# GpSimd takes the residual add of the combine stage, VectorE keeps the weighted sum and the gate

## The reference, cut to what matters

```python
out = jnp.zeros((T + 1, D), h.dtype).at[row_tok].add((yb * row_w[:, None]).astype(h.dtype))
...
x = x + gt2[:, None, :] * hier_moe(h2, router_grp_w[l], ...)
```

## Time and profile before

| what | value |
|---|---|
| median of three runs | 2645.95 us (2642.81 to 2648.5) |
| profiled execution | 2643.21 us |
| its span, first to last instruction | 2641.4 us |
| `combine`: first issue to the end of the span | 2564.4 to 2641.4 us |
| busy over the whole span | PE 90%, DVE 41%, ACT 29%, POOL 15% |

### The profile page before, as it was taken

The page is one execution under the profiler, slowest core; times in us unless marked ns, Lnnn a source line. Parts: engine busy times, 40 slices in busy tenths (PEclk is TensorE's granted clock), DMA queues, the critical chain, the costliest instruction groups (busy, mean ns, idle before and its releaser), DMA issues. The chain is left out here.

```text
span 2641.4 us, 67871 instructions
## 1 busy us (share of the span) xinstructions
PE 2384.7 (90%) x27948; PEld 1456.3 (55%) x27949; DVE 1095.7 (41%) x2600; ACT 761.1 (29%) x1879; POOL 389.9 (15%) x481
## 2 busy tenths in 40 slices
PE   6999999999996899999999997899999999999960
PEld 4787787877875667777776764332333323332220
DVE  1456565565654355555656556011111111111118
ACT  1444535445352123232232321121122212221212
POOL 1111211212111122121212210010110101100000
PEclk8999999999997899999999998799999999999985
DMA  9021211212118422222222222934545596999958
GB/s 342 19 87 49 97 49 69 77 49 97 49 71 330 167 94 90 106 90 106 74 97 91 91 74 89 419 148 192 209 142 231 200 363 247 387 387 388 391 217 365
DMA packets 54246, 451.84 MB, mean 171 GB/s; under 512 B 7884, under 2 KB 8944, under 8 KB 32528
## 3 DMA queue, kind: packets, MB, share of 16 engines
q1 hardware_dynamic: 37656, 391.25, 37.9%
q0 software_dynamic: 10656, 38.80, 3.8%
q10 hardware_dynamic: 5720, 18.66, 1.8%
HBM read 367.43 MB, written 87.56 MB: 172 GB/s over the span
## 5 line engine op out<-in xcount | busy, mean ns | idle before, releaser
L1833 PE MATMUL ps<-arena 128*32 128x512 f32 x4608 | 510.4, 600 | 26.4 <-DMA arena<-wex 26.4
L453 PE MATMUL ps<-arena 128*128 128x128 f32 x3072 | 354.8, 276 | 14.7 <-ACT arena L599 14.7
L453 PEld LDWEIGHTS ps<-arena 128*128 128x128 f32 x3072 | 349.3, 193 | 27.3 <-ACT arena L599 24.5
L1833 PEld LDWEIGHTS ps<-arena 128*32 128x32 f32 x4608 | 149.9, 111 | 379.9 <-issue 364.7
L1127 PE MATMUL ps<-arena 64*64 64x64 f32 x8704 | 298.0, 221 | 30.0 <-ACT arena L1362 9.5
L1127 PEld LDWEIGHTS ps<-arena 64*64 64x64 f32 x8704 | 276.9, 136 | 61.0 <-issue 60.3
L1847 PE MATMUL ps<-arena 128*32 128x512 f32 x2304 | 265.3, 601 | 8.9 <-DMA arena<-wex 7.9
L1272 PE MATMUL ps<-arena 128*128 128x512 f32 x480 | 222.0, 605 | 0.0
L2060 DVE TENSOR_TENSOR arena<-arena,ps 128x256 f32<-128x256 f32 x72 | 29.9, 415 | 462.3 <-ACT arena L1891 462.3
L468 PE MATMUL ps<-arena 128*128 128x512 f32 (+1 forms) x512 | 213.9, 555 | 0.0
L1891 ACT ACT_TABLE_LOAD x36 | 46.2, 1283 | 581.6 <-PE ps L1833 581.6
(11 more groups left out here) (350 smaller groups left out, 2871.9 us busy)
## 6 DMA issues: line engine op xcount, KB each, us to landing
arena<-wex SPq DMA_DIRECT2D x105, 2048.0 KB
mid<-arena SPq DMA_DIRECT2D x16, 2568.0 KB, 8.5
arena<-mid SPq DMA_DIRECT2D x16, 2568.0 KB, 9.8
arena<-ada SPq DMA_DIRECT2D x12, 2048.0 KB, 9.4
arena<-y SPq DMA_DIRECT2D x16, 1024.0 KB, 7.5
arena<-x SPq DMA_DIRECT2D x31, 512.0 KB, 5.8
arena<-x ACTq DMA_DIRECT2D x17, 512.0 KB, 10.3
arena<-w_in SPq DMA_DIRECT2D x4, 2048.0 KB, 39.5
```

The costliest lines, as they stand in the source:

```text
L453: mm = pe.matmul(bank[name][:, at:at + P], V["w_in"][g][:, kk, at:at + P], V["hT"][:, kk, :], start=(kk == 0), stop=(kk == KD - 1))
L1833: mm = pe.matmul(bank[("HA", "HB")[g]][rows[j], :], xT[:, kk, rows[j]], slot[j][:, at:at + 2 * FH], start=(kk == 0), stop=(kk == KD - 1))
```

## The change

The third operation of a tile moves from VectorE to GpSimd. VectorE's gated product goes to a new buffer of its own, `gated`, one for each of the four tiles in flight; these buffers lie in a part of SBUF that holds expert weights before and nothing in this stage.

The semaphore `gated` now tells that VectorE is done with `y0`, `y1` and `sum` of a tile. SyncE's loads and ScalarE's scaling wait for it where they waited for `summed`. GpSimd takes over the waits for x1 and for the store of tile t-4, and signals `summed`. VectorE waits for `summed` of tile t-4 before it writes `gated` again. The drain behind the gate goes.

```diff
+    W["gated"] = [W["slot"][FLIGHT // 2][:, PIECE + D * i:PIECE + D * i + D] for i in (1, 2, 3)] + [W["slot"][FLIGHT // 2][:, 2 * PIECE:2 * PIECE + D]]
...
                 if u:
-                    sp.wait_ge(S["summed"], t - FLIGHT + 1)
+                    sp.wait_ge(S["gated"], t - FLIGHT + 1)
...
                 dve.scalar_tensor_tensor(m["sum"], m["y1"], V["top_w"][:, 2 * t + 1:2 * t + 2], m["sum"], ALU.mult, ALU.add)
                 dve.drain()
-                dve.tensor_tensor(m["sum"], m["sum"], W["gt2"], ALU.mult)
-                dve.drain()
-                dve.wait_ge(S[f"x1_in{u}"], 16 * FLIGHT)
                 if u:
-                    dve.wait_ge(S[f"stored_out{b}"], 16 * u)
-                dve.tensor_tensor(m["res"], m["sum"], W["x1"][t], ALU.add).then_inc(S["summed"], 1)
+                    dve.wait_ge(S["summed"], t - FLIGHT + 1)
+                dve.tensor_tensor(m["gated"], m["sum"], W["gt2"], ALU.mult).then_inc(S["gated"], 1)
+
+        @block.gpsimd
+        def _(pool):
+            for t, b, u in tiles:
+                m = buf[b]
+                pool.wait_ge(S["gated"], t + 1)
+                pool.sem_inc(S["passed"], 1)
+                pool.wait_ge(S[f"x1_in{u}"], 16 * FLIGHT)
+                if u:
+                    pool.sem_inc(S["passed"], 1)
+                    pool.wait_ge(S[f"stored_out{b}"], 16 * u)
+                pool.tensor_tensor(m["res"], m["gated"], W["x1"][t], ALU.add).then_inc(S["summed"], 1)
...
             def scale(t, b, u):
                 act.wait_ge(S[f"y_in{b}"], 16 * u + 16)
                 if u:
-                    act.wait_ge(S["summed"], t - FLIGHT + 1)
+                    act.wait_ge(S["gated"], t - FLIGHT + 1)
```

More of the change, by code:

```diff
@@ L2075, in combine @@
     buf = [{n: w[:, D * i:D * i + D] for i, n in enumerate(("y0", "y1", "sum", "res"))} for w in W["flight"]]
+    for m, gated in zip(buf, W["gated"]):
+        m["gated"] = gated
     tiles = [(t, t % FLIGHT, t // FLIGHT) for t in range(NT)]
```

## The result

The changed kernel takes 2659.83 us (median of five runs, 2657.55 to 2662.81), the kernel before 2646.12 us in five runs beside it. The ratio is 1.0053, with a 95% interval of 1.0038 to 1.0068: about 14 us slower. Of the profiled executions, the span went from 2641.4 to 2655.7 us.

A forecast was written before the change was run, and what follows sets the result against it. VectorE was taken to bound combine at 3.86 us a tile. With exclusion, fifteen tiles at 4.56 us move the last add from 2638.25 to 2649.5, 11.2 us slower: median 2657 us, range 2648 to 2665.

The forecast's parts named there:

- The bound of before: Combine stage, first scaled tile on: VectorE's gate, add and weighted sum with drain set 3.86 us a tile.
- The exclusion: Combine: VectorE operations with two SBUF inputs and GpSimd's add block each other, the second waiting; forecast built on it 0.80.
- the second rival: Combine: only the plain product excludes GpSimd, the weighted sum doesn't; 2644 to 2649 us, centre 2646; chance 0.08.
- GpSimd's hold: Time GpSimd's 1024-column add blocks VectorE: 2.05 us, plus 0.14 until its end is seen; ends 1.91 and 2.38.
- The turns: Combine: VectorE and GpSimd alternate in an order differing within each pair of tiles; 9.11 us a pair, 4.56 a tile.
- The sum: Combine's end: fifteen tiles at 4.56 us put the last add's end at 2649.5, store 3.15 us; change costs 11.2 us.
- the first rival: Combine: no exclusion, GpSimd runs beside VectorE, DMA engines bound at 3.74 us a tile; 2644 us; chance 0.09.
- until 2630 the DMA engines are full: Combine before 2630 us: DMA engines at 413 to 426 GB/s, so a tile costs at least 3.74 us.

## Why the prediction was right

**The bound of before** (VectorE at 3.86 us a tile) was right: the run with the early release alone leaves VectorE's list and keeps the time.

**The exclusion** was the step that decided, and it was read from three rows of another stage and their sixteen repeats. Shown: the long sorts appear in the changed kernel on all three lines; they go when the second input of VectorE's operations leaves SBUF, and the time goes with them. The rule of the Trainium skill (SBUF — State Buffer, Who interferes with whom) holds, for the weighted sum too, which the rows of before couldn't show: it lasted up to 3.12 us. The block ends some 0.2 us ahead of the profiled end of GpSimd's add (2.14 of 2.34 us, below). With that the second rival, in which only the plain product excludes GpSimd, is refuted.

**GpSimd's hold** was put at 2.05 us. Measured: the weighted sum of 2607.62 ended at 2610.73; less its 1.28 it ran from 2609.45, and GpSimd had begun at 2607.31, so 2.14. The whole operation is 2.34, inside the ends of 1.91 and 2.38 and near the upper one: L1425's slope came near, L724's was too low (its 256-column row has 96 partitions, the other 128). For the whole operation my value was 2.05 + 0.14 = 2.19; the estimate from the Trainium skill (GPSIMD Engine Reference, Elementwise — side-by-side cycle accounting), 2.25, lies nearer to 2.34.

**The turns.** The predicted pair was 2.05 + 1.36 + 1.14 + 1.19 + 2.05 + 1.32 = 9.11 us; the measured one is 2.14 + 1.36 + 1.14 + 1.18 + 2.14 + 1.51 = 9.47 (1.18 is what the others leave of 9.47). The order is the predicted one, tile by tile, and the run with the scaling ahead shows that ScalarE's list sets it. Besides the hold, one term was mis-sized: from the end of a gate to the start of a free GpSimd I took 0.09 us, which no row of the prediction shows. The timeline of the stage has 0.18 for the first four tiles, and 0.28 from the fifth on (2603.83 + 3.20 = 2607.03 to 2607.31). The step comes where GpSimd's list gains its third wait, the one for the store, with a `sem_inc` of its own ahead of it; that these make it is argued only.

**The sum.** The last add ends at 2652.5 (2650.19 + 2.34) in place of the predicted 2649.5. 7.5 pairs at 0.36 more are 2.7 of these 3.0 us. The store behind it takes 3.15 us as before. So 14.3 us in place of 11.2, and 2659.8 in place of 2657, inside the range.

**What was off without harm: the first rival.** For a world with no exclusion I gave 1.7 us less than before. The run with PSUM is that world, and its stage is 4.3 us shorter. The failed step was "until 2630 the DMA engines are full": I took their share of 1.0 for it, while the rate, 386 to 426 GB/s, was VectorE's pace. At about 424 GB/s the loads end sooner (the last scaling starts 52.6 us after the first, in place of 56.0), and VectorE's backlog at the end is gone too. In the prediction itself this step set no term, since at 4.56 us a tile nobody asks that much of them.

## What to carry to other kernels

Before an elementwise operation goes to GpSimd, count VectorE's operations beside it that have two inputs in SBUF: GpSimd's time then adds to VectorE's, at 2.14 us held for 1.14 taken away here, and does not hide under it. Where one of VectorE's inputs can lie in PSUM (here ScalarE wrote it there at no cost), the same move becomes a gain: 14 us lost turn into some 6 won by the medians, 4.3 of them seen in the stage. A busy share of an engine or of the DMA engines that contains waits says little; compare single durations with the shortest of their kind, and GB/s with the highest that a stretch reaches.

## What the runs showed of the hardware

- An add of two float32 tiles of 128x1024 takes GpSimd 2.34 us alone (VectorE 1.23), a copy 1.04, a fill 0.95.
- The exclusion covers nearly the whole instruction (2.14 of 2.34 us of GpSimd's add), both ways: GpSimd waits for VectorE (3.12 in place of 2.34) and VectorE for GpSimd (3.20 in place of 1.23).
- VectorE's operations on 1024 columns take the same with one input in PSUM: 1288 against 1279 ns and 1225 against 1226 ns; ScalarE's scaling into PSUM takes 1117 against 1148 ns. One instruction may run over 1024 float32 columns of PSUM, twice the width of this program's own PSUM tensors.
- In the stretches of 10 us from 2580 to 2620 us, the DMA share reads 0.92 to 1.03 while the rate goes from 306 to 428 GB/s. The lowest pair is 0.92 at 306, in the run with the scaling ahead.
